# Summing the last four expert blocks of a layer by one-hot products on TensorE instead of through DRAM

## What is computed

```python
w = jnp.take_along_axis(scores, exp_idx, axis=-1)      # scores of the two chosen experts
w = w / jnp.sum(w, axis=-1, keepdims=True)
gates = jnp.einsum('tk,tke->te', w, jax.nn.one_hot(exp_idx, N_EXPERTS))
for e in range(N_EXPERTS):
    a = jax.nn.silu(h @ w_gate[e]) * (h @ w_up[e])
    y = y + gates[:, e:e + 1] * (a @ w_down[e])
# and around it: x += gate * moe(RMSNorm(x) * (1 + scale) + shift)
```

## Time and profile before

| | |
|---|---|
| median of 3 runs | 1158.22 us (1156.49 to 1161.33) |
| profiled execution, device time | 1159.45 us |
| its span, first to last instruction | 1157.5 us |
| mean granted TensorE clock | 0.952 of full speed |
| PE busy | 980.2 us (85%) |
| DVE / ACT / POOL busy | 404.5 / 365.1 / 217.8 us |
| DMA | 321.76 MB, mean 278 GB/s |

### The profile page before, as it was taken

How to read it: one execution, slowest core, us unless ns; L and a number is a source line. 1 busy time by engine, 2 the same in 40 slices (tenths; PEclk the granted TensorE clock), 3 DMA queues, 4 the chain that set the end, 5 groups by cost and what they waited for, 6 DMA issues and landing times.

```text
span 1157.5 us, 24481 instructions
## 1 busy us (share of the span) xinstructions
PE 980.2 (85%) x9648; PEld 656.2 (57%) x9649; DVE 404.5 (35%) x852; ACT 365.1 (32%) x777; POOL 217.8 (19%) x329
## 2 busy tenths in 40 slices
PE   5999999978899978898998569999999779976570
PEld 3677777544555655466666357887555545654340
DVE  2443330456733612122222373223753622212114
ACT  4432222566822222122222454224852111111011
POOL 0000000000000044244344202900000233432221
PEclk9999999999999999899999879999999899988896
DMA  9776666997320849999998476224437789999983
GB/s 356 260 279 218 218 219 213 318 375 296 118 101 37 328 168 422 421 422 423 421 424 369 162 237 164 73 73 166 198 119 298 279 347 420 423 423 424 425 365 116
DMA packets 92983, 321.76 MB, mean 278 GB/s; under 512 B 21305, under 2 KB 33250, under 8 KB 80626
## 3 DMA queue, kind: packets, MB, share of 16 engines
q1 hardware_dynamic: 84688, 304.53, 68.3%
q0 software_dynamic: 7008, 12.62, 3.0%
q10 hardware_dynamic: 1218, 3.62, 0.8%
HBM read 313.28 MB, written 13.99 MB: 283 GB/s over the span
## 4 chain that ended last, share of the span: by engine, by line
PE 68%; DMA 18%; DVE 5%; issue 4%; ACT 3%; SPq 1%; POOL 1%; ACTq 0%; POOLq 0%; DVEq 0%
PE ps L2030 23%; PE ps L1756 21%; DMA expert_sets<-in_moe_w_up_dram 12%; PE ps L1951 7%; PE ps L1669 5%; PE ps L1693 4%; PE ps L1710 2%; DMA ada_late<-in_ada_w_dram 2%; PE ps L1851 2%; PE ps L1878 1%; PE ps L1907 1%; DMA val<-expert_rows 1%; DMA expert_rows<-moe,scatter_idx 1%; PE ps L1829 1%; ACT hT L989 1%
## 5 line engine op out<-in xcount | busy, mean ns | idle before, releaser
L2030 PE MATMUL ps<-expert_sets,moe 128*32 128x256 f32 x6304 | 368.0, 394 | 81.9 <-DMA expert_sets<-in_moe_w_up_dram 40.9
L2030 PEld LDWEIGHTS ps<-expert_sets,moe 128*32 128x32 f32 x6304 | 236.7, 114 | 212.4 <-issue 104.5
L1596 DVE STREAM_TRANSPOSE moe<-moe 128x256 f32<-128x256 f32 x70 | 45.9, 656 | 305.8 <-PE ps L2030 287.8
L1756 PE MATMUL ps<-w_high,x_high 128*128 128x512 f32 x352 | 142.1, 404 | 5.1 <-DVE x_low L506 5.1
L1756 PE MATMUL ps<-w_low,x_high 128*128 128x512 f32 x352 | 138.8, 394 | 0.0
L1756 PE MATMUL ps<-w_high,x_low 128*128 128x512 f32 x352 | 138.8, 394 | 0.0
L1129 ACT ACTIVATE moe<-ps 128x128 f32<-128x128 f32 x68 | 18.9, 278 | 309.3 <-PE ps L2030 304.6
L489 DVE TENSOR_TENSOR w_low<-ring,w_high 128x2048 fp32r<-128x2048 f32 x24 | 57.0, 2377 | 133.0 <-ACT w_high L486 133.0
L781 POOL MEMSET moe<- 128x128 f32 x2 | 0.4, 204 | 530.9 <-PE ps L1977 530.9
L805 POOL DMA_INDIRECT expert_rows<-moe,scatter_idx x74 | 75.8, 1024 | 81.1 <-POOL scatter_idx L842 56.1
L1756 PEld LDWEIGHTS ps<-w_high,x_high 128*128 128x128 f32 x352 | 67.0, 190 | 30.0 <-issue 13.8
(11 more groups left out here) (247 smaller groups left out, 1085.0 us busy)
## 6 DMA issues: line engine op xcount, KB each, us to landing
expert_sets<-in_moe_w_down_dram SPq DMA_DIRECT2D x32, 2048.0 KB, 22.1
expert_sets<-in_moe_w_gate_dram SPq DMA_DIRECT2D x30, 2048.0 KB, 19.5
expert_sets<-in_moe_w_up_dram SPq DMA_DIRECT2D x30, 2048.0 KB, 24.7
ring<-in_ada_w_dram SPq DMA_DIRECT2D x16, 2048.0 KB, 8.1
ada_late<-in_ada_w_dram SPq DMA_DIRECT2D x6, 2048.0 KB, 13.2
ring<-in_na_w_qkv_dram SPq DMA_DIRECT2D x6, 2048.0 KB, 9.2
ring<-in_diff_w_qkv_dram SPq DMA_DIRECT2D x5, 2048.0 KB, 9.3
val<-expert_rows SPq DMA_DIRECT2D x12, 512.0 KB, 4.5
```

The source lines that it names most:

```text
L1596: dve.transpose(blk_inT, blk_in[b].rearrange("p (j k) -> p k j", k=KC)).then_inc(m_xt[l], 1)
L1756: mm = pe.matmul(ps[:, job_bank(l, n)], x_part[:, k, tok], w_part, start=(k == 0 and i == 0), stop=(k == KC - 1 and i == 2))
L2030: mm = pe.matmul(ps[g * SLOTS:(g + 1) * SLOTS, bank, 0:n_out], lhs_T[:, k, :], weights(k, g), start=(k == 0), stop=(k == n_chunks - 1), sk ...
```

## The change

The blocks are divided into those that are looped over, `2 * (pairs - 2)` of them, and the last four, whose code is written out.

- The last four blocks' rows are not scattered. DVE multiplies them by the layer's gate and stores them as full rows of 1024 in `last_rows`, 32 rows for each block (four instructions of 32 partitions for each block). DVE makes `last_marks`, a one-hot matrix of slot and token weighted with the router's weight. PE multiplies marks and rows into PSUM, for the first two tiles on top of the residual rows that are there already.
- The other blocks' rows are read back while the last four run, by SP, both choices of all tiles at once (a new buffer `y_second`). Ahead of that POOL scatters zeros to the rows that the last four blocks would have written (four scatters, in one stretch).
- The first strip of layer 1's weights is loaded behind these reads.
- In layer 0 the layer's gate is applied to each block (`gate_now`, made for each block from the context gate and the difference to the latent one), by DVE instead of ACT; the combine step loses its gate product.
- PE puts the first two residual tiles into PSUM (identity products) instead of ACT. A second table product gives each slot its weight (`slot_share`); the counts of `keep_busy` fall by what was added.
- At the end ACT splits both halves of the strip behind all its `weigh_first`; DVE splits one half ahead of `norm1` and one behind it.

```diff
+                looped = pool.value_load(plan[0:1, 0:1], ...)
...
+                with pool.Fori(1, looped) as j:
+                    next_pair(j, 0)
+                pool.tensor_copy(scatter_idx[:, 2:2 + LAST], slot_idx[:, bass.ds(2 * looped + BLK_COLS, LAST)]).then_inc(m_ix[l], 1)
+                pool.wait_ge(m_ix[l], 4 * looped + 3)
                 in_turn()
-                for b in range(2):
-                    pool.wait_ge(m_y[l], 2 * pairs + b)
-                    in_turn()
-                    scatter(b, (blk_out[0], blk_last)[b], 2 + b)
+                for i in range(LAST):
+                    scatter(i, blk_none, 2 + i, s_zero)
+                next_pair(looped, 1)
...
+            def load_expert_rows(l):
+                for p, used, more in ((N_EXP - 2 - l, m_gu, 0), (N_EXP - 3, m_dn, 1)):
+                    blocks = sp.value_load(plan[0:1, p + 1:p + 2], ...)
+                    sp.wait_ge(used[l], blocks + more)
+                looped = sp.value_load(plan[0:1, 0:1], ...)
+                sp.wait_ge(s_zero, 16 * LAST * (l + 1))
                 for b in range(2):
-                    sp.wait_ge(m_sc[l][b], pairs * 16 + 16 + 16 * b)
+                    sp.wait_ge(m_sc[l][b], looped * 16 + 16 + 16 * b)
-                for m, t in enumerate(TILES_OF[l]):
-                    if m >= 2:
-                        sp.wait_ge(s_cb[l], m - 1)
-                    for k in range(2):
-                        sp.dma_start(val[:, 2 * (m % 2) + k], src).then_inc(s_yl[l][m % 2], 16)
+                for m in range(NT[l]):
+                    for k, rows_to in enumerate((val, y_second[l])):
+                        sp.dma_start(rows_to[:, m], src).then_inc(s_yl[m], 16)
...
-            last_blocks, n0 = load_experts(0)
+            load_experts(0)
+            load_expert_rows(0)
+            last_blocks = sp.value_load(plan[0:1, N_EXP - 1:N_EXP], ...)
             sp.wait_ge(m_dn[0], last_blocks + 1)
             load_strip(1, 0)
-            load_expert_rows(0, n0)
...
+                def gate_block_out(j, b, last=None):
+                    if l == 0:
+                        stt(gate_now, gate_late, slot_late[:, bass.ds(2 * j + b, 1)], gate_tile, ALU.mult, ALU.add).then_inc(m_gate, 1)
+                        dve.wait_ge(m_gate, 2 * j + b + 1)
+                    if last is None:
+                        dve.wait_ge(m_sc[l][1 - b], 16 * j + 16)
+                        tt(blk_out[1 - b], ps[:, 5, 0:DG], gates, ALU.mult).then_inc(m_y[l], 1)
+                        return
+                    for g in range(GROUPS):
+                        part = slice(g * SLOTS, (g + 1) * SLOTS)
+                        made = tt(last_rows[last * SLOTS:(last + 1) * SLOTS, g * DG:(g + 1) * DG], ps[part, 5, 0:DG], gates[part], ALU.mult)
+                    made.then_inc(m_y[l], 1)
...
+                with dve.Fori(0, looped) as j:
+                    for b in range(2):
+                        block_steps(j, b)
+                block_steps(looped, 0)
+                mark_last()
+                block_steps(looped, 1, 0)
+                block_steps(looped + 1, 0, 1)
+                block_steps(looped + 1, 1, 2)
+                add_stored(l, 0)
+                dve.wait_ge(m_dn[l], 2 * looped + 2 * 2 + 1)
+                gate_block_out(looped + 1, 2, 3)
+                add_stored(l, 1)
+                add_last(l, 0)
+                add_last(l, 1)
                 if l == 0:
-                    for half in range(2):
-                        split_weights(dve, 1, 0, half)
-                if l == 0:
-                    for m in range(2):
-                        add_experts(0, m)
+                    split_weights(dve, 1, 0, 0)
                     for t in range(CTX_TILES):
                         norm1(1, t)
+                    split_weights(dve, 1, 0, 1)
...
+            def add_stored(l, m):
+                dve.wait_ge(s_w1, MADE[l] + m + 1)
+                step(stt(val[:, m], y_second[l][:, m], wts[:, 1, m:m + 1], val[:, m], ALU.mult, ALU.add))
+                if m >= 2:
+                    step(tt(val[:, m], val[:, m], resid[:, TILES_OF[l][m]], ALU.add))
+            def add_last(l, m):
+                dve.wait_ge(s_comb, SUMMED[l] + m + 1)
+                lo, hi = sum_banks(m)
+                sync(tt(resid[:, TILES_OF[l][m]], val[:, m], ps[:, lo:hi + 1].rearrange("p a b -> p (a b)"), ALU.add), s_cb)
...
                 pe.wait_ge(m_y[l], 2 * pairs + 1)
+                pe.wait_ge(s_tok, l + 1)
+                for m in range(NT[l]):
+                    if m == 3:
+                        pe.wait_ge(s_cb, 2)
+                    for h in range(2):
+                        mm = pe.matmul(ps[:, sum_banks(m)[h]], last_marks[:, m * P:(m + 1) * P], last_rows[:, h * HALF:(h + 1) * HALF],
+                                       start=(m >= 2), stop=True, skip_group_check=True)
+                    mm.then_inc(s_comb, 1)
```

More of the change, by code:

```diff
@@ L151, in build_trunk @@
         w_high = [over(f"w_high_{i}", SET_KB[0] + 16 + 8 * i, [P, KC // 2, STRIP], F32R) for i in range(3)]
+        y_second = [over(f"y_second_{l}", (SET_KB[1] + 16, SET_KB[0])[l], [P, TILES, D]) for l in range(LAYERS)]
         small_in = over("small_in", SET_KB[0] + 40, [P, D])
@@ L328, in build_trunk @@
         s_hs = sem("head_squares")
-        s_w1 = [sem(f"first_experts_weighed_{l}") for l in range(LAYERS)]
+        s_w1 = sem("first_experts_weighed")
         s_ot = [sem(f"o_turned_{l}") for l in range(LAYERS)]
@@ L829, in _, with next_pair @@
                     gather(b)
-                with pool.Fori(1, pairs) as j:
+                def next_pair(j, before):
                     for b in range(2):
@@ L934, in _ @@
                     stream_in(act, 1, 0)
-                    for m in range(CTX_TILES, TILES):
-                        weigh_first(0, m)
                     for t in range(CTX_TILES, TILES):
-                        act.wait_ge(s_cb[0], t + 1)
+                        act.wait_ge(s_cb, t + 1)
                         norm1(1, t)
@@ L1176, in _ @@
             tt, ts, stt = dve.tensor_tensor, dve.tensor_scalar, dve.scalar_tensor_tensor
-            step(dve.memset(plan[:, 0:1], 0))
             dve.wait_ge(s_vec_t, 2)
@@ L1279, in _ @@
                     for t in range(CTX_TILES, TILES):
-                        add_experts(0, t)
+                        add_stored(0, t)
+                        add_last(0, t)
                     for t in range(CTX_TILES, TILES):
@@ L1559, in _ @@
                 tt(here, here, dest.unsqueeze(3).to_broadcast([P, 2, nt, BLK_COLS]), ALU.mult).then_inc(s_oh[l], 1)
+                dve.wait_ge(s_oh[l], 2)
+                for k in range(2):
+                    shared = stt(slot_share[:, k * nt:(k + 1) * nt], here[:, k], 0.0,
+                                 wts[:, k, 0:nt].unsqueeze(2).to_broadcast([P, nt, BLK_COLS]), ALU.is_gt, ALU.mult)
+                shared.then_inc(s_oh[l], 1)
                 dve.wait_ge(s_tab[l], 1)
@@ new lines, in mark_last @@
+                def mark_last():
+                    for i in range(LAST):
+                        part = slice(i * SLOTS, (i + 1) * SLOTS)
+                        step(dve.tensor_copy(last_token[part].unsqueeze(1), slot_token[part, bass.ds(2 * looped + i, 1), :]))
+                    step(stt(token_at[:, 0:NT[l]], const("block")[:, 0:NT[l]], -float(P), last_token[:, 0:1].to_broadcast([P, NT[l]]),
+                             ALU.mult, ALU.add))
+                    dve.wait_ge(s_comb, SUMMED[l])
+                    for m in range(NT[l]):
+                        marked = ts(last_marks[:, m * P:(m + 1) * P], ps[:, 3, 0:P], token_at[:, m:m + 1], last_token[:, 1:2],
+                                    ALU.is_equal, ALU.mult)
+                    marked.then_inc(s_tok, 1)
@@ L2105, in _ @@
                     ends.append(expert(p, ends[p - 1], ends[p], then=p + 1 if p < 3 else None))
+                pe.matmul(ps[:, 3, 0:P], one, const("before"), start=True, stop=False)
+                pe.matmul(ps[:, 3, 0:P], one, ident, start=False, stop=True).then_inc(s_comb, 1)
                 with pe.Fori(0, (N_EXP - 4) // 3 - l) as three:
```

183 lines of the change are left out of this document (97 added, 86 removed).

## The result

The changed kernel takes 1163.3 us (median of 20 runs, 1158.45 to 1169.65) where the kernel before takes 1160.18 (20 runs, 1154.21 to 1164.78). The ratio is 1.0033, 95% interval [1.0018, 1.0047]: no faster, and if anything a third of a per cent slower. I had forecast 8.3 us less. The profiled execution of the changed kernel took 1166.05 us, its span is 1163.8 us and its mean granted clock 0.946.

What follows compares the result with a forecast made beforehand. Expert weight loads bound the loops, with PE idle behind both; -4.5 (layer 0's end) - 4.7 (layer 1's end) + 0.2 + 0.7 = -8.3 us from 1158.22 gives 1149.9 us, range 1147.5 to 1152.4.

Steps and rivals of the forecast that it cites:

- It reaches nothing else but the start of the phases: Whole kernel: besides both layers' ends, the change touches only the start of the experts' phases; other stages 0.
- The term ahead of the first gather (+0.2): Start of the experts' phases: an extra plan value ahead of a POOL step that layer 0 waits for, +0.2 us.
- Layer 1's end, "4.7 us": Behind layer 1's loop: the last scale starts at 1148.5 instead of 1153.20, 4.7 us gained.
- Layer 0's end, "-4.5": Behind layer 0's loop: PE starts layer 1 at 668.8 instead of 673.27, 4.5 us gained.
- What is ready last is no longer the last block but the strip: Layer 0's end: the strip, loaded behind the row reads, lands at 659.7 and sets the end; DVE alone is ready sooner.
- Zeros, "I cost this at nothing": Layer 0's loop: four zero scatters delay a gather by 5.1 us; the weights' wait covers it, cost 0.
- the first sign that the prediction gave for being wrong: Layer 0's last blocks: PE waits for `moe<-h_rows`; no size given.
- Layer 1's stream, "+0.7": Layer 1's loop: the zero scatters' bytes lie ahead of the last weights and cost 0.7 us.
- It doesn't do what it says: Rival: row reads can't start before PE's end, the strip lands at 672, layer 0 loses 7.5; 1162 us, chance 0.05.
- starved gathers: Rival: zeros on POOL's queue delay block n-2's gather 23.6 us, PE stands 15 us or more; 1166 us, chance 0.08.

Runs made afterwards that it cites:

- e6: The changed kernel with PE's first wait set to DVE's counted step 1 instead of 2; 1158.24 us, 0.9996 of the kernel before.
- b2: The kernel before with PE's first wait set to DVE's counted step 3 instead of 2; 1161.45 us, 1.0018 of the kernel before.
- c_before: The kernel before, unaltered, run once more for a second profile; 1160.19 us.
- b1: The kernel before with each block of layer 1's loop evicted by four multiplications of 32 partitions; 1161.4 us, 1.0029 of the kernel before.
- e2: The changed kernel with the early ones of the last four blocks evicted whole, then copied in parts; 1158.75 us, 0.9999 of the kernel before.
- before: The kernel before, unaltered, in its earlier profile, the one the prediction was made from; median of 20 runs 1160.18 us.
- e4: The changed kernel with unread products keeping PE busy ahead of the one-hot products; 1157.49 us, 0.9990 of the kernel before.
- e7: The changed kernel with e1, e2, e4 (9 products in layer 1), e6 and DVE's last eviction before its first stored-row sum; 1150.62 us, 0.9936 of the kernel before.
- e1: The changed kernel with 5 (layer 0) and 4 (layer 1) fewer keep-busy products; 1160.19 us, 1.0010 of the kernel before.
- e3: The changed kernel with POOL's four zero scatters issued at the start of the loop; 1162.43 us, 1.0028 of the kernel before.
- e8: The changed kernel with POOL's four zero scatters moved behind the gather of block n-2; 1162.19 us, 1.0031 of the kernel before.
- e0_after: The changed kernel again, unaltered, in a second set of runs with a profile; 1160.5 us, 1.0019 of the kernel before.

## Why the prediction was wrong

It was wrong by 10 to 12 us: -8.3 forecast, +2 to +4 measured. The mechanism was right and is in the profile: rows are read before PE's end, and both ends get shorter. The sum had the start at nothing, left out PE's waits for evictions in parts, and took the strip for the only path that sets layer 0's end.

- **"It reaches nothing else but the start of the phases": failed, +2.5 us.** The change also took away a counted step ahead of everything, and a wait on that count was left as it was. Undone in e6 (386.50) and made in the kernel before in b2 (389.40): shown in both directions in the profiles, by PE's first product and by the means over 14 profiles (386.8 and 389.8), though neither total alone excludes zero. The term ahead of the first gather (+0.2) was small as forecast (18.1 us before, 17.8 after, where the rank product is not delayed); the step that failed is that the whole start of the kernel stood at zero in the sum.
- **Layer 1's end, "4.7 us": mis-sized, it gave 1.8.** Of its parts, PE's end to the last scale came nearly as forecast: 1153.20 - 1134.0 = 19.2 before (18.8 in `c_before`), 14.5 forecast, 15.3 and 15.6 measured (four parts take 1.73 us, not 1.4). But I took PE's end as fixed at 1134.1, and it is later: 24.8 and 26.7 us behind the first product with the last up weights before, 27.4 and 27.6 after. The four parts hold PE up ahead of the next down products by 1.3 us, which b1 shows in the kernel before; in e2 PE's end comes at 25.5 us. The lower clock on the last down products is in both kernels (3.43 us in `c_before`, 3.64 and 3.22 after, 1.92 only in `before`). So the earlier trace rows held the best of three profiles of this stretch (24.8 us; the others have 26.0 and 26.7), and part of the difference to it is not the change's. That the products ran at half clock (5.08 us for 8) was foreseen; e4 and e7 show what it is worth.
- **Layer 0's end, "-4.5": reached in two of four profiles, where two paths end together.** From the first product with the last up weights to PE's first transpose it is 39.4 us before, in both profiles; the forecast has 34.9; measured are 37.7 and 34.6, and 36.3 and 34.6 in e1 and e6, which leave this code as it is. "What is ready last is no longer the last block but the strip" is the step that failed: in all four the transpose comes 5.2 us behind DVE's second `add_last`, which ends within 0.5 us of ACT's split in the good profiles, 1.2 us behind it in e1 and 3.2 us behind it in the first (671.5 against 664.53 + 3.70 = 668.2). That path is longer than I had it for two reasons. PE's last down products start 3.1 us later than before and not 1.0: 0.9 by the wait of 1.20 us ahead of the gates (0.30 before), 2.2 by the eviction in parts (2.81 us, 0.59 before), which I had put at nothing. And the products behind these waits are not always at full clock: the one-hot products take 7.11 us in the two good profiles, 8.80 in the other two, and in the first the last down products take 3.31 for 1.93. Why the clock falls behind the same waits in one profile and not in another stays open.
- **Zeros, "I cost this at nothing": failed in its place, hardly in the sum.** The gather took 7.8 us to land, not under 6, and PE stood 1.20 us instead of 0.30; this is close to the first sign that the prediction gave for being wrong, only that PE waited for the gathered rows by way of DVE. But in e3 the wait is gone and the time stays. e8 can't tell, since it delays the last scatter and with it the row reads.
- **Layer 1's stream, "+0.7": +2.9 up to the last up weights.** 1.5 us of it are between the last router product and the rank product (9.8 instead of 8.3 us in both profiles of the changed kernel and in e6; but 8.3 in e2, e3, e4 and e8 too, which leave that code as it is, and 10.0 in b2, so not clearly the change's). The zeros are 0.7 by the prediction's estimate, which no run measures by itself. The rest, about 1 us, is open. So is the +1.1 of layer 1's mixer, which varies from 222.8 to 224.7 with the granted clock in variants of both kernels.

Of the rivals none is what happened. "It doesn't do what it says" is nearest in its time (1162 us), but SP read the rows at 646.04, 16 us before PE's end; "starved gathers" named the place at which DVE did wait, but PE lost 0.9 us there and not 15. e7's 1150.62 us is by chance close to the forecast 1149.9: it holds repairs of layer 1's end that gain more than the forecast had there, against a stream that costs more.

## What to carry to other kernels

When a diff removes or adds an instruction that counts up a semaphore, look up every engine that waits on a number of that count: the wait doesn't fail, it just means another instruction, and here it cost a third of what the change was to gain. When the work between two products of PE is split into smaller instructions, cost it at the place where PE waits for it, with the clock that PE has after that wait. When two chains end within a few us of each other, price the end by both. And take a second profile of the kernel before ahead of the forecast: here the stretch from the last weights to PE's end differs by 1.9 us between two profiles of one kernel, as much as the effect that was looked for in it.

## What the runs showed of the hardware

- A DVE multiply of 32 partitions by 256 columns takes as long as one of 128 by 256: 0.42 to 0.44 us against 0.38 to 0.42 us. I had taken 0.35. The Trainium skill (VectorE: DVE Perf Modes, Why `tensor_reduce` can't reduce along partition axis) says that DVE streams along the free dimension with a lane of its own for each partition; the rows agree.
- 32 down products of PE take 1.93 us behind waits of 2.81 (`e0_after`, layer 0) and 2.87 us (e2), and 3.64 behind one of 4.12 us (changed kernel), with a granted clock of 0.50. But it is 3.31 behind the same 2.81 us (changed kernel, layer 0), 3.46 behind 3.21 (b1), 3.43 behind 4.33 (`c_before`), 1.92 behind 2.94, and 3.57 behind 2.11 us in e7, where PE had stood before that too. The length of the last wait alone doesn't tell which level it will be, and the level is worth 1.4 to 1.7 us.
- An indirect gather of 32 rows, issued behind four indirect scatters while the weights stream, landed 7.8 us after its issue. In layer 1 of the changed kernel two gathers with no zeros just ahead of them took 6.8 us under the stream, so most of this time is not the zeros'.
